# Moving a norm step, a gate product and the S2 sums of a layer kernel to other slots

## The reference, cut to what matters

```python
h = rmsnorm(x, ln_gain[l])
proj = h @ w_in[l]
q_a, k_a, v_a, g_a, b_c, c_c, x_c, g_c, q_m, g_m = jnp.split(proj, offsets, axis=-1)
o_a = swa_sink_attention(q_a, k_a, v_a, q_norm_a[l], k_norm_a[l], sinks[l], bias)
o_c = short_gated_conv(b_c, c_c, x_c, conv_w[l])
mem_h = rmsnorm(mem, mem_ln_gain[l])
o_m = memory_cross_attention(q_m, mem_h, w_mem_kv[l], q_norm_m[l], k_norm_m[l])
mixed = jnp.concatenate([jax.nn.silu(g_a) * o_a, jax.nn.silu(g_c) * o_c,
                         jax.nn.silu(g_m) * o_m], axis=-1)
x = x + mixed @ w_out[l]
```

## Time and profile before

| | |
|---|---|
| median of three runs | 2602.19 us |
| the profiled execution, its own time | 2601.53 us |
| its span in the profile | 2599.7 us |
| PE busy | 2572.8 us (99%) |
| DVE busy | 1783.1 us (69%) |
| POOL busy | 1775.2 us (68%) |
| ACT busy | 1271.3 us (49%) |
| mean granted TensorE clock | 0.999 of full |

### The profile page before, as it was taken

One profiled execution on the slowest core, in us unless ns is written; L12 is line 12 of the kernel. 1 busy time (PEld: TensorE's weight loads), 2 busy tenths in 40 slices (PEclk: granted clock), 3 DMA queues, 4 the chain that ended last, 5 costly groups with the idle time before them and its releaser, 6 DMA issues.

```text
span 2599.7 us, 33898 instructions
## 1 busy us (share of the span) xinstructions
PE 2572.8 (99%) x12092; PEld 2127.0 (82%) x12092; DVE 1783.1 (69%) x2217; ACT 1271.3 (49%) x2661; POOL 1775.2 (68%) x1238
## 2 busy tenths in 40 slices
PE   8999999999999999999999999999999999999999
PEld 6888888888887888878888888878888888878887
DVE  4457674576745757457577868788488785888677
ACT  7455454545544555445554554544444454454443
POOL 6587667876677856778545676777476676776666
PEclk9999999999999999999999999999999999999999
DMA  8576767777677776676777443355655444334533
GB/s 262 165 270 219 241 177 246 251 226 242 180 240 250 234 231 193 232 258 214 237 203 229 142 155 101 97 170 178 194 164 156 149 140 135 93 106 151 178 125 137
DMA packets 323852, 492.27 MB, mean 189 GB/s; under 512 B 17942, under 2 KB 134756, under 8 KB 317540
## 3 DMA queue, kind: packets, MB, share of 16 engines
q1 hardware_dynamic: 209076, 299.25, 37.8%
q10 hardware_dynamic: 114608, 190.85, 21.6%
HBM read 367.61 MB, written 97.25 MB: 179 GB/s over the span
## 4 chain that ended last, share of the span: by engine, by line
PE 91%; DVE 4%; POOL 2%; DMA 1%; ACT 1%; SPq 1%; issue 0%; ACTq 0%
PE acc L1780 14%; PE acc L1782 13%; PE acc L1781 13%; PE acc L1852 7%; PE acc L1854 7%; PE acc L1856 7%; PE ps_s L1852 2%; PE ps_s L1854 2%; PE ps_t L1852 2%; PE ps_z L1852 2%; PE ps_s L1856 2%; PE ps_o L1852 2%; PE ps_t L1854 2%; PE ps_z L1856 2%; PE ps_o L1856 2%; PE ps_z L1854 2%
## 5 line engine op out<-in xcount | busy, mean ns | idle before, releaser
L737 POOL TENSOR_TENSOR w_lo<-raw,w_hi 128x512 fp32r<-128x512 f32 x896 | 1262.7, 1421 | 753.3 <-ACT w_hi L862 747.2
L862 ACT ACTIVATE w_hi<-raw 128x512 fp32r<-128x512 f32 x896 | 557.1, 629 | 874.1 <-PE acc L1782 369.8
L1780 PE MATMUL acc<-w_hi,h_hi 128*128 128x512 f32 (+1 forms) x1024 | 374.7, 366 | 3.8 <-POOL w_lo L737 3.8
L1782 PE MATMUL acc<-w_hi,h_lo 128*128 128x512 f32 (+1 forms) x1024 | 371.6, 363 | 0.0
L1781 PE MATMUL acc<-w_lo,h_hi 128*128 128x512 f32 (+1 forms) x1024 | 371.5, 363 | 0.0
L1780 PE MATMUL acc<-h_hi,w_hi 128*128 128x512 f32 x768 | 311.0, 405 | 0.0
L1782 PE MATMUL acc<-h_hi,w_lo 128*128 128x512 f32 x768 | 299.6, 390 | 0.0
L1781 PE MATMUL acc<-h_lo,w_hi 128*128 128x512 f32 x768 | 299.4, 390 | 0.0
L1661 DVE TENSOR_TENSOR a_lo<-s_sum,a_hi 128x512 fp32r<-128x512 f32 x192 | 219.4, 1175 | 36.8 <-ACT a_hi L1148 33.3
L1780 PEld LDWEIGHTS acc<-w_hi,h_hi 128*128 128x128 f32 x1024 | 193.3, 189 | 36.9 <-POOL w_lo L737 5.5
L1782 PEld LDWEIGHTS acc<-w_hi,h_lo 128*128 128x128 f32 x1024 | 193.3, 189 | 30.2
(11 more groups left out here) (277 smaller groups left out, 5416.4 us busy)
## 6 DMA issues: line engine op xcount, KB each, us to landing
raw<-in_w_in SPq DMA_DIRECT2D x256, 512.0 KB, 4.6
raw<-w_sums SPq DMA_DIRECT2D x128, 512.0 KB, 3.8
w_sums<-stage ACTq DMA_DIRECT2D x32, 1024.0 KB, 5.3
probs_t<-blocks_t SPq DMA_DIRECT2D x384, 64.0 KB, 2.9
raw<-in_w_out SPq DMA_DIRECT2D x48, 512.0 KB, 3.6
stage<-in_w_in ACTq DMA_DIRECT2D x32, 512.0 KB, 5.4
h_rows<-early ACTq DMA_DIRECT2D x16, 1024.0 KB, 7.4
half_rows<-ungated ACTq DMA_DIRECT2D x16, 1024.0 KB, 8.5
```

The costliest lines, as they stand in the source:

```text
L737: nc.gpsimd.tensor_tensor(w_lo[:, at, :], raw[:, slot_mod, HALF * half:HALF * half + HALF], w_hi[:, at, :].bitcast(F32), ALU.subtract).the ...
L862: nc.scalar.activation(w_hi[:, 2 * (slot_mod % 2) + half, :], raw[:, slot_mod, HALF * half:HALF * half + HALF], ACT.Copy).then_inc(hi_read ...
L1780: nc.tensor.matmul(dst, st[0], mv[0], start=first, stop=False)
L1782: return nc.tensor.matmul(dst, st[1], mv[0], start=False, stop=last)
```

## The change

It does four things.

1. In the first stage POOL takes the inverse root of tile 3 (`x_item`) ahead of the remainders of slot 13, where it took it behind them. The separate table for that goes.
2. In slot 12 of each group DVE multiplies tile 2 by its gain (`x_gain`) behind the first part of the query scaling and turning, where it did so ahead of it.
3. After a gating pair POOL mixes block c12 in slots 2 and 3 of the next pair, where it did so in slots 5 and 6.
4. For the output pairs 2 and 6 DVE makes S2 in slots 26 and 27 of the pair before and in slots 1 and 2, where it did so in slots 1 to 4. Pairs 0 and 4 keep slots 1 to 4.

```diff
-LAST_MIX_AT = {0: ("c21", 2, 4), 5: ("c12", 0, 2), 6: ("c12", 2, 4)}
+LAST_MIX_AT = {0: ("c21", 2, 4), 2: ("c12", 0, 2), 3: ("c12", 2, 4)}
+S2_OUT_AT = {(1, 26): 0, (1, 27): 1, (2, 1): 2, (2, 2): 3}
...
-X_RSQRT_AT = {4: 0, 7: 1, 10: 2}
-X_RSQRT_LATE_AT = {13: 3}
+X_RSQRT_AT = {4: 0, 7: 1, 10: 2, 13: 3}
...
-                    if s in X_RSQRT_LATE_AT:
-                        x_item(2 + TT + g * TT + X_RSQRT_LATE_AT[s])
...
-                    if s in X_GAIN_FIRST_AT:
-                        x_gain(g, X_GAIN_FIRST_AT[s])
...
-                if r % 2 == 0 and 1 <= at <= PRODUCT_SLOTS:
+                if r % 4 == 0 and 1 <= at <= PRODUCT_SLOTS:
                     s2_tiles(r, at - 1)
+                if (r % 4, at) in S2_OUT_AT:
+                    s2_tiles(r + r % 2, S2_OUT_AT[r % 4, at])
```

More of the change, by code:

```diff
@@ L152 @@
 X_SQUARE_AT = {3: 0, 6: 1, 9: 2, 12: 3}
-X_RSQRT_AT = {4: 0, 7: 1, 10: 2}
-X_RSQRT_LATE_AT = {13: 3}
+X_RSQRT_AT = {4: 0, 7: 1, 10: 2, 13: 3}
 X_SCALE_AT = {5: 0, 8: 1, 10: 2, 14: 3}
 X_FLIP_AT = {5: 0, 8: 1, 10: 2, 14: 3}
-X_GAIN_AT = {6: 0, 9: 1, 15: 3}
-X_GAIN_FIRST_AT = {12: 2}
+X_GAIN_AT = {6: 0, 9: 1, 12: 2, 15: 3}
 H_STORE_AT = {7: 0, 10: 1, 13: 2, 16: 3}
```

## The result

The changed kernel takes 2634.28 us, the median of four runs (2632.32 to 2636.37), the one before 2601.86 us in the same comparison (2600.66 to 2602.44). The ratio is 1.0127, with a 95% interval from 1.0114 to 1.0140: the change makes the kernel 1.3% slower. The forecast was 2636, in a range from 2612 to 2645.

The account below looks back on a forecast made before the run. PE is busy for 99% of the span, so a step on another engine counts only where PE waits for it. The terms 9.2 + 20.6 + 4.8 = 34.6 us on 2601.5 us gave 2636 us, range 2612 to 2645.

Parts of the forecast that it names:

- The root and the gain: First stage, four groups: root waits for a mean now behind the gain, PE restarts 2.3 us later each, 9.2 us.
- The held root: First stage, POOL: the root starts just behind DVE's second query scaling, is held, and ends at 161.4.
- c12 in pairs 1 and 5: Second stage: the four products run on POOL where DVE has idle time, 0 us.
- S2: Second stage, pairs 2 and 6: DVE's remainders come late at slots 1, 2, 4 and 5; 20.6 us for both.
- The clock: Clock falls behind PE's waits: two of four in the first stage, one more in pair 6; 4.8 us (0 to 8).
- Rival 1: Losses overlap or tail milder: POOL rests in slots 3 to 5 of pairs 2 and 6; 2616 to 2620, chance 0.15.
- Rival 2: The change wins: DVE's idle time ahead of slot 1 takes early halves of S2; 2599 or 2590, chance 0.05.

Follow-up runs that it names:

- run 1: Kernel before with only the two first-stage moves (root of tile 3 earlier, gain of tile 2 later): 2614.84 us against 2600.50.
- run 5: Kernel before with only the S2 calls of pairs 2 and 6 moved, c12 staying in slots 5 and 6: 2610.55 us, ratio 1.0041.
- run 9: Kernel before with only S2 of pairs 2 and 6 split, subtractions in slot n and additions in slot n + 1: 2596.58 us against 2600.59.
- run 2: Kernel before with only the two second-stage moves (c12 in slots 2 and 3, S2 in slots 26, 27, 1, 2): 2620.77 us, ratio 1.0078.
- run 8: Kernel before with the gain of tile 2 behind the first query turns and S2 of pairs 2 and 6 split: 2593.52 us, ratio 0.9974.

## Why the prediction was right

Step by step:

- **The root and the gain, 9.2 us.** Measured 8.6 (12.4 - 3.8 us of waiting in run 1). The chain was the one foreseen: root behind mean, mean behind gain. The mean came within 0.1 us of the forecast.
- **The held root.** Foreseen by a neighbour's 0.92 us to take about 1.6 us; it took 1.47.
- **c12 in pairs 1 and 5, 0 us.** PE has no wait there in the changed kernel.
- **S2, 20.6 us.** Slots 1, 2, 4 and 5 of pair 2 were forecast 3.9, 4.0, 0.6 and 4.9 us late, and were 4.0, 3.8, 0.1 and 4.3. The pace of 1.71 us an operation held. Slots 4 and 5 were a little better since POOL waited for its weights twice in that stretch. In pair 6 slots 1, 2, 3 and 5 were 4.0, 3.8, 1.7 and 2.2 us late. Less the old 3.1 us a pair that is about 17.7 us, so the term was 3 us too large.
- **The clock, 4.8 us.** This term was too small: 8.7 us by the profile, beyond its stated upper bound of 8. In the first stage I took two falls in four. All four waits of 3.1 us had one, in the full change and in run 1, and the profile of the change has 5.9 us for them and not 3.2. In the second stage there is one more fall behind the last late slot, as forecast, and the one that was there already has grown, together 2.8 us and not 1.6. That the falls between the late slots hide in the next wait came true. "TensorE: Matmul & The Clock Gate" of the Trainium skill (HAM oscillation — how this bites in real kernels) tells of a cold start after every wait; for the first stage of this kernel the trace agrees, with four of four. For waits of 2.6 us the traces do not: before has one fall in two and run 1 none.
- **Rival 1** (POOL rests in the tail) was half a mechanism: run 5 shows what it would give, 10.0 us for both pairs, if c12 stayed away. **Rival 2** had the right lever, idle time of DVE ahead of slot 1, at the wrong place: run 9 uses DVE's idle time between the remainders of slots 2 and 3 and wins 4.0 us.

In the profiled execution the three terms measure 8.6, 17.7 and 8.7 us, about 35 us, against a forecast of 9.2 + 20.6 + 4.8 = 34.6. The mechanisms were right; that the total comes out this close is luck, as an S2 term too large and a clock term too small cancel. The stages by themselves say the same: forecast at 12.4 and 22.2, they cost 14.3 and 20.3 in runs 1 and 2. By the medians the full change costs 32.4 us.

## What to carry to other kernels

Where PE is busy for 99% of the time, a moved step is to be judged by what now stands behind it on its own engine and by what it waits for itself: a root of 0.55 us ahead of a 2.5 us step cost 14 us in four groups, because its input came last on another engine and the operation behind that input held the root. Look for the idle time on the engine itself, and move work in pieces that fit it; two operations fitted where four did not. Count moves together where they land in the same slots: the early c12 products, which cost 2.7 us alone, cost 10 us beside the moved S2.

## What the runs showed of the hardware

Beside what was forecast, the holding between DVE and POOL has a second form. In the pairs above the two engines took turns, one operation of 128x512 each in 1.71 us. In the version of run 8 DVE was already running through operations without a pause when POOL came, and POOL got no turn. The first fence is DVE's timeline there, the second POOL's line 737 between 1690 and 1710 us (shortest, median, longest in ns).

```profile
1696.86 1.28 DVE L1675 TENSOR_TENSOR ungated<-ungated,half_top 128x512 f32<-128x512 f32 x2
1698.06 1.28 DVE L1661 TENSOR_TENSOR a_lo<-ungated,a_hi 128x512 fp32r<-128x512 f32 x2
1699.26 1.28 DVE L1680 TENSOR_TENSOR ungated<-ungated 128x512 f32<-128x512 f32 x2
```

```profile
L737 POOL TENSOR_TENSOR w_lo<-raw,w_hi x7: 1292/1734/5154, 1688.8 to 1708.8; 128x512 fp32r<-128x512 f32 x7
```

One remainder took 5.15 us, from 1696.53 until after DVE's run had ended at 1700.5, while the DVE operations kept their 0.6 us. PE then waited 0.8 us for it. The same remainder took 5.15 us in pairs 2 and 6 of run 8 and again in both pairs of run 9, four of four, so it is no accident of one execution. What decides which form comes up was not tried and stays open.

The eleven profiles together, from 100 us on, also say when the granted clock fell to the lower of its two levels, 1.2 GHz. After waits of PE of 3.0 us and more it fell in 21 of 21 cases (0.50 to 0.71 over the 5 us behind the wait), after those of 2.5 to 2.7 us in 8 of 12, and after those of 0.7 to 1.5 us in none. After the three waits of 1.9 to 2.2 us it fell each time, but these stand 7 to 18 us behind another wait with a fall of its own. Two profiles of kernels that are alike in a stretch can so differ by 1.6 us for each wait of 2.6 us in it, which is as much as some of the differences above.
